# A fixed order of small operations and weight conversions for each pair of experts, and an eighth place for raw weights

## The reference, cut to what matters

```python
xs = xt[slot_tok].reshape(n_blocks, MOE_BLOCK, D)
def expert_block(args):
    xb, e = args
    a = xb @ w_gate[e]          # 1024 x 512
    u = xb @ w_up[e]            # 1024 x 512
    return (jax.nn.silu(a) * u) @ w_down[e]   # 512 x 1024
...
ys = ys * slot_gate[:, None]
out = jnp.zeros((T, D), ys.dtype).at[slot_tok].add(ys)
```

## Time and profile before

| what | value |
|---|---|
| median of 2 runs | 1769.42 us (1769.29 to 1769.56) |
| profiled execution | 1774.48 us, span of its instructions 1772.7 us |
| mean granted PE clock over the span | 0.944 |
| PE, DVE, ACT busy over the span | 90%, 59%, 41% |
| loads of expert units | 192 of 1024 KB |

### The profile page before, as it was taken

One profiled execution on the slowest core, in us unless ns is written; L12 is line 12 of the kernel. 1 busy time (PEld: TensorE's weight loads), 2 busy tenths in 40 slices (PEclk: granted clock), 3 DMA queues, 4 the chain that ended last, 5 costly groups with the idle time before them and its releaser, 6 DMA issues.

```text
span 1772.7 us, 20410 instructions
## 1 busy us (share of the span) xinstructions
PE 1590.5 (90%) x8032; PEld 1179.6 (67%) x8032; DVE 1054.0 (59%) x1353; ACT 727.9 (41%) x943; POOL 260.5 (15%) x180
## 2 busy tenths in 40 slices
PE   6999999999999999999999998977777777777774
PEld 4778866679889899998877887644444444444442
DVE  6636777876677475658998657544444444444442
ACT  6424255534435344435332556433333333333432
POOL 0000030000283323000000001111111111111101
PEclk9999999999999999999999999988898888988886
DMA  7316701022224231412210139887887777877873
GB/s 319 119 68 250 286 3 70 1 96 95 95 72 143 72 143 48 143 42 102 84 59 24 54 135 365 323 302 302 315 315 302 298 298 296 314 283 308 322 290 130
DMA packets 54069, 322.90 MB, mean 182 GB/s; under 512 B 11490, under 2 KB 12514, under 8 KB 17362
## 3 DMA queue, kind: packets, MB, share of 16 engines
q1 hardware_dynamic: 43584, 307.91, 45.1%
q0 software_dynamic: 8256, 8.42, 2.3%
q10 hardware_dynamic: 2130, 5.22, 0.8%
HBM read 319.67 MB, written 19.14 MB: 191 GB/s over the span
## 4 chain that ended last, share of the span: by engine, by line
PE 69%; DMA 15%; DVE 8%; ACT 5%; SPq 2%; issue 2%; POOL 0%; POOLq 0%; DVEq 0%; ACTq 0%
PE ps L613 23%; DMA raw<-in_experts 13%; PE ps L1536 8%; PE ps L1128 7%; DVE wlo L2386 4%; PE ps L803 4%; ACT whi L1679 4%; PE ps L1559 4%; PE ps L1384 2%; PE ps L1051 2%; PE ps L779 2%; PE ps L836 1%; SPq L3565 1%; DMA xT<-in_x 1%; PE ps L915 1%
## 5 line engine op out<-in xcount | busy, mean ns | idle before, releaser
L2386 DVE TENSOR_TENSOR wlo<-raw,whi 128x2048 fp32r<-128x2048 f32 x166 | 384.2, 2318 | 427.8 <-ACT whi L1679 426.3
L1679 ACT ACTIVATE whi<-raw 128x2048 fp32r<-128x2048 f32 x166 | 315.8, 1907 | 426.0 <-DMA raw<-in_experts 328.3
L1536 PE MATMUL ps<-raw,xS 128*64 128x512 f32 x240 | 143.3, 753 | 102.2 <-DVE xS L2496 102.2
L1536 PEld LDWEIGHTS ps<-raw,xS 128*64 128x64 f32 x240 | 38.4, 172 | 187.3 <-DVE xS L2496 108.1
L1537 PE MATMUL ps<-raw,xS 128*64 128x512 f32 x240 | 143.2, 753 | 0.0
L613 PE MATMUL ps<-hH,whi 128*128 128x512 f32 x352 | 138.6, 394 | 0.3 <-ACT dmax L2166 0.3
L613 PE MATMUL ps<-hH,wlo 128*128 128x512 f32 x352 | 137.1, 389 | 0.0
L613 PE MATMUL ps<-hL,whi 128*128 128x512 f32 x352 | 137.0, 389 | 0.0
L1591 PE MATMUL ps<-whi,xH 128*128 128x512 f32 x272 | 110.9, 408 | 5.2 <-DVE xL L2499 4.2
L1591 PE MATMUL ps<-whi,xL 128*128 128x512 f32 x272 | 106.3, 391 | 0.0
L1591 PE MATMUL ps<-wlo,xH 128*128 128x512 f32 x272 | 106.1, 390 | 0.0
(11 more groups left out here) (580 smaller groups left out, 3783.5 us busy)
## 6 DMA issues: line engine op xcount, KB each, us to landing
raw<-in_experts SPq DMA_DIRECT2D x192, 1024.0 KB, 8.4
raw<-in_streamed SPq DMA_DIRECT2D x92, 1024.0 KB, 4.8
xT<-in_x SPq DMA_DIRECT2D x1, 2048.0 KB, 17.6
sum_scratch<-xN ACTq DMA_DIRECT2D x2, 1024.0 KB, 8.7
Y<-sum_scratch SPq DMA_DIRECT2D x4, 512.0 KB, 5.0
out<-Y SPq DMA_DIRECT2D x4, 512.0 KB, 2.8
h_scratch<-hN SPq DMA_DIRECT2D x4, 384.0 KB, 2.6
ctxT<-in_ctx SPq DMA_DIRECT2D x1, 1024.0 KB, 17.8
```

The lines of the kernel that those rows point to most:

```text
L1536: e.matmul(b.t[0:64, :], xS[:, kk, :], g.raw[:, k, :], start=(kk == 0), stop=(kk == 7), tile_position=(0, 0))
L1679: e.activation(u.hi, u.raw, ACT.Copy).then_inc(*p.inc("hi", n, on="hi"))
L2386: e.tensor_tensor(u.lo, u.raw, u.hi.bitcast(F32), ALU.subtract).then_inc(*p.inc("lo", n, on="lo"))
```

## The change

It makes three edits. (1) The ring of raw places gets an eighth place (PH + 10240), taken in at x = 3, whose first load waits for `perm` of DVE; the final gains `fgb` and the tile `sgS` move out of its way. (2) From x = 2 on, ACT and DVE follow an order written out per pair: `upto(n)` converts exactly up to unit n, and the small operations stand between. (3) In the turns of x = 0 and 1 `use_split` no longer runs past u2.1. PE's program, POOL's program and the order of loads stay.

```diff
@@ units
+        if x == 3:
+            raw_ring.append(Place(PH + 10240))
...
+    EIGHTH = min(u.n for u in units if u.place == PH + 10240 and u.n > U_OUT2[3])
...
-    fgb = at("fgb", PH + 11264, [1024])
+    fgb = at("fgb", O_HH + 3072, [1024])
...
-    sgS = at("sgS", O_HH + 3072, [4, 64])
+    sgS = at("sgS", O_HH + 1536, [4, 64])
@@ act_program and dve_program
         def use_split(n):
-            while split_at[at_[0] - 1] < min(split_at[n] + 3, len(split_order) - 1):
+            while split_at[at_[0] - 1] < min(split_at[n] + 3, split_at[U_E["u", 2][1]]):
                 convert(at_[0])
+
+        def upto(n):
+            while at_[0] <= n:
+                convert(at_[0])
@@ act_program, the loop from x = 2 (before: one loop over all x with use_split)
+        for x in range(2, NEXP, 2):
+            nx = x + 1
+            more = nx + 1 < NEXP
+            if x == 8:
+                p.wait_ge(*done("pe", "use", U_E["u", 1][1]))
+                e.dma_start(fgb, A["final_rows"]).then_inc(*p.land("fg"))
+            upto(U_E["d", x][0])
+            turned(x)
+            upto(U_E["d", x][1])
+            if more:
+                turn_x(x + 2)
+            paired(nx)
+            if more:
+                upto(U_E["g", x + 2][1])
+                gated(x)
+                sigmoid_small(nx)
+                upto(U_E["u", x + 2][0])
+                sigmoid(x + 2)
+                upto(U_E["u", x + 2][1])
             else:
-                use_split(U_E["d", x][1])
-                sigmoid(x + 1)
-            gated(x)
-        gated(NEXP - 1)
+                sigmoid_small(nx)
+                gated(x)
+            gated(nx)
@@ dve_program, the loop from x = 2
+        for x in range(2, NEXP, 2):
+            nx = x + 1
+            more = nx + 1 < NEXP
+            silu(x)
+            upto(U_E["d", x][0])
+            lower_a(x)
+            upto(U_E["d", x][1])
+            if more:
+                turn_x(x + 2)
+                upto(U_E["g", x + 2][1])
+            silu_small(nx)
+            if more:
+                upto(U_E["u", x + 2][0])
+                turn_small(nx + 2)
+                upto(U_E["u", x + 2][1])
@@ sp_program
-            if n == FIFTH:
+            if n in (FIFTH, EIGHTH):
                 p.wait_ge(*done("dve", "perm"))
```

More of the change, by code:

```diff
@@ L2326, in act_program @@
         sigmoid(0)
[L2327 to L2338, removed]
+        for x in range(2):
+            for n in U_E["u", x]:
+                use_split(n)
+            if x:
+                use_split(U_E["g", x + 1][0])
+            turned(x)
             use_split(U_E["g", x + 1][0])
@@ L2341, in act_program @@
             use_split(U_E["d", x][0])
-            if x + 2 < NEXP and not small(x + 2):
-                turn_x(x + 2)
-            if small(x + 1):
-                paired(x + 1)
-                use_split(U_E["d", x][1])
-                if x == NEXP - 2:
-                    sigmoid_small(x + 1)
-            else:
-                use_split(U_E["d", x][1])
-                sigmoid(x + 1)
-            gated(x)
-        gated(NEXP - 1)
+            if x == 0:
+                turn_x(2)
+            use_split(U_E["d", x][1])
+            sigmoid(x + 1)
+            gated(x)
[6 more added lines that the diff above has]
+            upto(U_E["d", x][0])
+            turned(x)
+            upto(U_E["d", x][1])
+            if more:
+                turn_x(x + 2)
+            paired(nx)
[6 more added lines that the diff above has]
+                upto(U_E["u", x + 2][1])
+            else:
+                sigmoid_small(nx)
+                gated(x)
+            gated(nx)
         p.stage("over")
@@ L3338, in silu_small @@
             TT(aS, sgS, v[:, :, 64:128], ALU.mult, "aL", x)
-        for x in range(NEXP):
-            if small(x):
-                silu_small(x)
-            else:
[L3344 to L3358, removed]
+        for x in range(2):
+            use_split(U_E["u", x][0])
+            silu(x)
+            use_split(U_E["u", x][1])
+            if x:
+                use_split(U_E["g", x + 1][0])
+            else:
+                permute()
+            lower_a(x)
+            use_split(U_E["g", x + 1][0])
+            use_split(U_E["g", x + 1][1])
+            use_split(U_E["d", x][0])
+            (turn_small if x else turn_x)(x + 2)
+            use_split(U_E["d", x][1])
+        for x in range(2, NEXP, 2):
+            nx = x + 1
+            more = nx + 1 < NEXP
+            silu(x)
+            upto(U_E["d", x][0])
+            lower_a(x)
+            upto(U_E["d", x][1])
[7 more added lines that the diff above has]
+                upto(U_E["u", x + 2][1])
         p.stage("over")
```

## The result

| | before | after |
|---|---|---|
| median | 1769.42 us | 1633.11 us (1632.62 to 1633.61) |
| ratio, 95% interval | | 0.923 (0.919 to 0.9269) |
| profiled execution, its span | 1774.48, 1772.7 us | 1633.61, 1631.8 us |
| end of `pair(3,0)` to end of `pair(31,0)` | 1126.0 to 1737.0, 611.0 us | 1125.8 to 1595.2, 469.4 us |

The kernel is 136.3 us faster by the medians, 140.9 by the two profiled executions. The stretch of 14 pairs alone gives 141.6, so all of it is there: 43.6 us a pair became 33.5.

What follows compares the result with a forecast made beforehand. PE and DMA both waited in a closed loop through `xS`. With it gone, DMA's floor of 475 us, less 3, takes the stretch from 611 to 472: 1769.4 - 139 = 1630 us, range 1600 to 1672 for 8 in 10.

Steps and rivals of the forecast that it cites:

- xS stands behind d16.0's conversion: In DVE's order, the `xS` copy waits behind an unrelated load's conversion; PE's 102.2 us wait goes wholly if the rest keeps up.
- aS: PE's wait ahead of `down_small`: 28.1 us goes, except a fraction, once ACT's narrow sigmoid stands ahead of u16.0's conversion.
- Clock: PE's work at 1.2 instead of 2.4 GHz costs 49.4 us in the stretch; nearly all of it goes with the long gaps.
- g16.0 at 0.3 us a pair: PE reaches g16.0 at 10.8, its conversion is ready at 11.1: 0.3 a pair, 4 us in all, bounds 0 and 14.
- The eighth place: In the ring of raw places, waits move to loads wanted later, so the ring no longer stands in PE's loop.
- DMA as the floor, 388 GB/s, 475 us less 3: Over the 14 pairs, 184.45 MB at 388 GB/s take 475 us; loads already 3 us ahead make it 472.
- A: Rival: PE is last, not DMA, whose rate rises to 420 GB/s; 440 us for the stretch, 1598 in all; chance 0.14.
- B: Rival: PE and DMA limits hit each other, half-clock spells in each pair; 36 to 38.5 a pair, 1662 to 1697; chance 0.15.
- E: Rival: the burst's DMA rate doesn't last, 352 GB/s is the limit; 524 us for DMA, kernel 1682; chance 0.06.
- C: Rival: the wait only changes its name, PE stops for d16.1's or g18.0's conversion; 1735 to 1769; chance 0.04.
- D: Rival: slower, as a pair's six conversions no longer run ahead; 1797 at 15 us exposed a pair; chance 0.03.
- SP's waits on the matmuls of pairs: Sign named for the forecast being right: in SP's queue these waits come to under 100 us in all.

Runs made afterwards that it cites:

- experiment 3: The changed kernel with the copy of `xS` alone put back behind the conversion of the next pair's first down unit: 1726.61 us, ratio 0.9741.
- experiment 2: The kernel before with the eighth place added and the old order of ACT and DVE kept: 1727.3 us, ratio 0.9744.
- Experiment 4: The kernel before with the copy of `xS` alone moved ahead of the conversion of the next pair's first down unit: 1748.32 us, ratio 0.9861.
- experiment 6: The kernel before with conversions running two converted units ahead instead of three, in both engines: 1703.64 us, ratio 0.9617.
- experiment 7: The changed kernel with the narrow expert's sigmoid alone put back behind the conversion of the first up unit: 1635.13 us, ratio 0.9219.
- experiment 1: The changed kernel with the eighth place taken out, so the new order with seven places: 1636.73 us, ratio 0.9239.
- experiment 8: The changed kernel with half of each narrow expert's second up unit from x = 5 on not loaded, TensorE's work kept: 1619.38 us, ratio 0.9133.
- experiment 9: The changed kernel with two of four steps in the second half of narrow gate and up products left out from x = 5 on: 1635.52 us, ratio 0.9226.
- experiment 10: The changed kernel with scatters of 32 rows instead of 128 from x = 4 on: 1609.18 us, ratio 0.908.
- experiment 5: The kernel before with conversions running one converted unit ahead instead of three from x = 2 on, in both engines: 1737.99 us, ratio 0.9817.

## Why the prediction was right, step by step

**The fault.** *xS stands behind d16.0's conversion.* Shown by experiment 3: putting this one copy back gives up 93 of the 136 us, and the 43 that are left are about what the place alone gives (45, experiment 2). Experiment 4 adds what the prediction only assumed when it let the 102.2 go "wholly, if the rest keeps up": with the copy alone moved, the rest does not keep up, and the load next to it, d16.1, stops `turn_a` instead. It takes the copy and the products for `ac` ahead of d16.0's and d16.1's conversions (experiments 3, 4 and 6); the narrow sigmoid isn't needed there (experiment 7), and of the wide one no run tells by itself.

**aS.** *28.1 goes.* It went to 0.0. But moving the sigmoid was worth nothing in the changed kernel: experiment 7 puts it back and loses no time. In the old order the eighth place alone takes the wait away (0.7 in experiment 2), which the prediction didn't see. The 28.1 counted in the prediction's sum only as part of the difference of two stretches, so that the total wasn't hurt.

**Clock.** *Nearly all of the 49.4.* Busy time is 441.9 against 427.7 of full-clock work, so 14.2 stayed and 35.2 went. The 14.2 cost nothing in the end, for DMA was the bound: with 8 us less of it experiment 7 is no faster.

**g16.0 at 0.3 us a pair.** Not seen: the idle time on `xL` and `wlo` is nil. The wait came one step earlier, at `down`, where I had 2.9 us to spare for d16.0. That margin was worked out with a landing time of 7.45, read where the queues had nearly run empty. In full queues the load takes 13.4, and by the chain above this is the place where TensorE's 27.5 us of idle time lies, 2.0 a pair for the 3 forecast.

**The eighth place.** *The ring no longer stands in PE's loop.* True, but true for seven places as well (experiment 1), and the prediction didn't ask that. The wait it credits to the place is taken away by the order.

**DMA as the floor, 388 GB/s, 475 us less 3.** This carried the sum. Measured: 389 GB/s at share 0.99 over 469 us, a difference of 3 us from 472. Experiments 8 and 9 show that it is the bound and not merely busy. Choosing the rate of one fully busy stretch of 17 us over the 370 GB/s of the dense row was the step that decided between 1630 and 1654. Its basis was narrow: in the changed kernel the rate of a fortieth of the stretch (11.7 us) goes from 332 to 424 GB/s once DMA is full, so that 17 us could have shown a rate some per cent off. That DMA would be the bound was reasoned; that this rate met the mean of 469 us within 1 GB/s was in part luck.

**The rivals.** A needed 420 GB/s with scatters in the stream; experiment 10 reaches 406 with part of them out. B's half-clock spells did come, in 10 of the 14 pairs, but in TensorE's slack. E falls: 389 GB/s lasted for 469 us. The Trainium skill, "DMA: Bandwidth & Descriptors", section Specifications, gives about 358 GB/s as a core's limit; the measured rate lies above it, with one core running alone. C and D had no trace in the changed kernel, though experiments 4 and 5 are C, waits that change their names at 1748 and 1738 us. The one sign that I had named and that missed is SP's waits on the matmuls of pairs, 112.1 for "under 100".

## What to carry to other kernels

In an engine with a strict order, ask of each small operation which load the instruction ahead of it may await; a copy of 0.7 us behind the wrong conversion cost 93 us here, because it closed a loop from TensorE over the release of a place to the next load. Moving that one alone wasn't enough (24 us), and neither was a shorter lookahead (33 and 68 us of the 136): look for the next operation in the loop that stands behind the same load. For the gain, take the next floor rather than the sum of the waits that go: bytes over the rate of a stretch in which DMA never rested gave 472 of 469 us, while the waits and the clock loss together had been 183.

## What the runs showed of the hardware

- Loads of 1 MB beside gathers and scatters ran at 389 GB/s for 469 us on a core alone, and at 406 with part of the scatters left out. The scatters are small in bytes (7 MB of 183 with the gathers) but cost more DMA time than their bytes: leaving out 2556 packets with 1.8 MB gave 24 us.
- TensorE's granted clock still fell to 0.50, or 1.2 GHz, for a short spell in 10 of the 14 pairs (1333.5 to 1336.7, say), each time at the end of an idle time of 1.9 to 3.1 us or just after it; its mean over the stretch is 0.96. In experiment 7, with six idle times of 1.9 to 3.6 us, there were two such spells, and the mean is 0.99.
- A fuller DMA queue shows in each load's time, 16.5 us from issue to landing in the median for 8.5 before, while the rate rose from 302 to 389 GB/s. The landing time of 7.45 us, read behind nearly empty queues, was no price for a load in full ones, which took 13.4.
